# Norm weights as one value per partition behind the transposes, and pooling matrices kept on chip, in a two-block transformer kernel

## The reference, cut to what matters

```python
def first_block(x, c, ...):                      # two layers
    mod = cond @ w_ada[l] + b_ada[l]             # sh1, sc1, g1, sh2, sc2, g2
    h = rms_norm(x, norm1_g[l]) * (1.0 + sc1) + sh1
    proj = h @ w_in[l]                           # pooled part p, and q, k, v
    pooled = windowed_means(p) - p               # windows 2, 4, 8, 16
    pool_out = einsum('bsgc,gcd->bsgd', pooled, pool_w[l]) * pool_scale[l]
    y = rms_norm(concat(pool_out, attn_out), per half of 512) * mix_norm_g[l]
    x = x + g1 * (y @ w_out[l])
    h2 = rms_norm(x, norm2_g[l]) * (1.0 + sc2) + sh2
    x = x + g2 * peer_ffn(h2, ...)               # 128 of 16384 experts a token
def second_block(x, ...):                        # two layers
    proj = rms_norm(x, norm1_g_2[l]) @ w_in_2[l]
    mix = concat(rms_norm(y_a, out_g_mla), y_b, rms_norm(y_c, out_g_swa), rms_norm(y_d, out_g_na))
    x = x + mix @ w_out_2[l]
    x = x + relu(rms_norm(x, norm2_g_2[l]) @ w_up[l])**2 @ w_down[l]
    # at the end rms_norm(x, final_norm_g)
```

## Time and profile before

| | |
|---|---|
| time, median of 3 runs | 2333.84 us (2329.98 to 2336.41) |
| the profiled execution: time, span | 2331.16 us, 2329.4 us |
| PE busy | 2084.4 us (89%) |
| DVE busy | 1346.7 us (58%) |
| ACT busy | 820.0 us (35%) |
| POOL busy | 613.9 us (26%) |
| bytes moved by DMA | 760.73 MB, mean 327 GB/s |

### The profile page before, as it was taken

How to read it: one execution, slowest core, us unless ns; L and a number is a source line. 1 busy time by engine, 2 the same in 40 slices (tenths; PEclk the granted TensorE clock), 3 DMA queues, 4 the chain that set the end, 5 groups by cost and what they waited for, 6 DMA issues and landing times.

```text
span 2329.4 us, 24219 instructions
## 1 busy us (share of the span) xinstructions
PE 2084.4 (89%) x8172; PEld 1235.6 (53%) x8172; DVE 1346.7 (58%) x3055; ACT 820.0 (35%) x2346; POOL 613.9 (26%) x564
## 2 busy tenths in 40 slices
PE   6888998888989888999888888889989999999998
PEld 5554554434545434655433343436756667766665
DVE  2237766985767677776776676754533323444323
ACT  2214643554454344463443344442420001331000
POOL 1124534334334443433444344430000000000000
PEclk9999999999999899999999999999999999989999
DMA  9999999999999999999999999994342442242430
GB/s 374 365 408 426 426 426 427 427 426 427 426 427 411 427 427 417 427 426 427 420 426 403 426 427 427 420 423 169 127 181 109 184 184 77 109 162 93 190 142 18
DMA packets 106848, 760.73 MB, mean 327 GB/s; under 512 B 12114, under 2 KB 12386, under 8 KB 15843
## 3 DMA queue, kind: packets, MB, share of 16 engines
q0 software_dynamic: 80640, 587.24, 60.3%
q1 hardware_dynamic: 26084, 171.94, 18.5%
HBM read 758.08 MB, written 1.05 MB: 326 GB/s over the span
## 4 chain that ended last, share of the span: by engine, by line
PE 52%; DMA 25%; DVE 14%; ACT 6%; issue 2%; POOL 0%; DVEq 0%; ACTq 0%; POOLq 0%
PE PS L541 51%; DMA BIG<-in_uv,EID 22%; DVE BIG L1716 6%; DMA MOD<-in_uv,EID 2%; ACT DG L1018 1%; DMA BIG<-in_wada 1%; ACT L1224 1%; DVE BIG L1378 1%; DVE BIG L1388 1%; PE PS L653 1%; DVE SC L1464 1%; ACT AV L1018 1%; PE PS L620 1%; DVE BIG L1374 1%; DVE X L1378 1%
## 5 line engine op out<-in xcount | busy, mean ns | idle before, releaser
L541 PE MATMUL PS<-BIG,DG 128*128 128x512 f32 x1820 | 891.9, 628 | 157.6 <-ACT DG L1018 138.2
L1716 DVE CUSTOM_DVE_ANT_0 BIG<-BIG,H 128x1024 f32<-128x1024 f32 x455 | 558.1, 1227 | 321.7 <-DMA BIG<-in_uv,EID 292.0
L481 POOL DMA_INDIRECT BIG<-in_uv,EID x455 | 519.4, 1142 | 738.8 <-PE PS L541 708.2
L541 PEld LDWEIGHTS PS<-BIG,DG 128*128 128x128 f32 x1820 | 334.6, 197 | 615.0 <-ACT DG L1018 298.4
L541 PE MATMUL PS<-HT,BIG 128*128 128x128 f32 (+1 forms) x2304 | 382.2, 322 | 7.9 <-DVE HT L1374 3.5
L541 PEld LDWEIGHTS PS<-HT,BIG 128*128 128x128 f32 x2304 | 348.4, 192 | 74.0 <-issue 46.6
L1224 ACT ACTIVATE AV<-AV 128x1 f32<-128x1 f32 x512 | 103.1, 201 | 635.8 <-DVE AV L1716 632.0
L541 PE MATMUL PS<-BIG,HT 128*128 128x256 f32 (+3 forms) x1216 | 295.9, 400 | 7.8 <-DVE HT L1374 3.6
L541 PEld LDWEIGHTS PS<-BIG,HT 128*128 128x128 f32 x1216 | 227.1, 193 | 74.6 <-issue 48.1
L1378 DVE TENSOR_TENSOR BIG<-BIG 128x256 f32<-128x256 f32 (+2 forms) x176 | 96.2, 546 | 221.7 <-ACT BIG L1359 216.5
L1018 ACT ACTIVATE DG<-CST,AV 128x128 f32<-128x128 f32 x512 | 205.5, 401 | 48.0 <-ACT AV L1018 0.7
(11 more groups left out here) (179 smaller groups left out, 1448.2 us busy)
## 6 DMA issues: line engine op xcount, KB each, us to landing
BIG<-in_wada POOLq DMA_DIRECT2D x43, 1024.0 KB
BIG<-in_wup SPq DMA_DIRECT2D x32, 1024.0 KB, 8.9
BIG<-in_wdn SPq DMA_DIRECT2D x32, 1024.0 KB, 4.8
BIG<-in_win SPq DMA_DIRECT2D x31, 1024.0 KB, 4.9
BIG<-in_wq SPq DMA_DIRECT2D x27, 1024.0 KB
BIG<-in_wout SPq DMA_DIRECT2D x24, 1024.0 KB, 5.4
BIG<-in_uv,EID POOLq DMA_INDIRECT x455
MOD<-in_wada POOLq DMA_DIRECT2D x5, 1024.0 KB
```

Of the source, the lines that this page charges most:

```text
L481: pool.e.indirect_dma_start(out=slot(u), out_offset=None, in_=I[f"uv{l}"], in_offset=bass.IndirectOffsetOnAxis(ap=EID[:, t * 128 + j:t * 1 ...
L541: return pe.e.matmul(dst, a, b, start=start, stop=stop)
L1716: v.e.tensor_tensor_reduce(out=JD, in0=slot(u)[:, 0:1024], in1=H[:, t, :], scale=1.0, scalar=0.0, op0=ALU.mult, op1=ALU.add, accum_out=AV[ ...
```

## The change

Most norm weights no longer stand as rows on all partitions. They come in one small transfer (`in_cols`, 128 x 112) as columns, one value per channel with channels on partitions, and the copies behind a transpose multiply by them, since there the channel is the partition. DVE's norm then needs two operands only (`ts` instead of `stt`). ACT's copy of four 128-wide pieces in one instruction becomes four instructions, each with its own column as scale; its copy of a 256-token section pair becomes two. DVE's copy becomes one `tensor_tensor` with the columns spread along the free dimension. `par1` shrinks to 648 values per partition, `par2` to 516. The first block's second norm weight is multiplied into the modulation: in layer 0 as a row loaded to `JS`, in layer 1 on the small tile `ROWS`. The pooling matrices get a place of their own (`MGB`), loaded once for both layers, and `poolw` one (`PWB`), loaded once a layer. The two operands of the modulation matmuls move from `PARB` to `DG` and `TC`.

```diff
-PAR = 3720
+PAR = 792
...
-P1 = dict(n1=(0, 1024), n2=(1024, 1024), ps=(2048, 512), qg=(2560, 64), kg=(2624, 64), sink=(2688, 8), mg=(2696, 1024))
-P2 = dict(n1=(0, 1024), n2=(1024, 1024), q=(2048, 192), kv=(2240, 128), lam=(2368, 128), sub=(2496, 64), sink=(2560, 4),
-          oa=(2564, 256), oc=(2820, 256), od=(3076, 256))
+P1 = dict(ps=(144, 512), qg=(656, 64), kg=(720, 64), sink=(784, 8))
+P2 = dict(q=(144, 192), kv=(336, 128), lam=(464, 128), sub=(592, 64), sink=(656, 4))
+
+GAINS = dict(mg=(80, 8), n1=(96, 8), n2=(112, 8), mix=(128, 8))
...
-        DG = sb("DG", 4 * 128)[:, :].rearrange("p (b n) -> p b n", b=4)
+        DGS = sb("DG", 4 * 128)[:, :]
+        DG = DGS.rearrange("p (b n) -> p b n", b=4)
...
-        ZC = PARB[:, 384:888].rearrange("p (k m) -> p k m", k=8)
-        CREP = PARB[:, 128:384].rearrange("p (k m) -> p k m", k=8)
+        MGB = sb("MGB", 1536)[:, :]
+        PWB = sb("PWB", 512)[:, :]
+        N2R = sb("N2R", 256)[:, :]
+        ZC = DGS[:, 0:504].rearrange("p (k m) -> p k m", k=8)
+        CREP = TC.rearrange("p (k m) -> p k m", k=8)
...
+        def columns(k, l, c, n=4):
+
+            o, w = GAINS[k]
+            return PARB[:, o + l * w + c:o + l * w + c + n]
...
+        GAIN_OF = {(l, 1): ("mg", l) for l in range(L)} | {(2 + l, w): (("n1", None, "n2")[w], l) for l in range(L) for w in (0, 2)}
...
-                    sp.e.dma_start(PARB[:, 1024:PAR], I["par1"][1, 1024:PAR].partition_broadcast(128)).then_inc(*landed("ld_par", 1))
+                    sp.e.dma_start(PARB[:, 144:PAR], I["par1"][1].partition_broadcast(128)).then_inc(*landed("ld_par", 1))
...
-                        sp.e.dma_start(PARB[:, 1024:PAR], I["par1"][0, 1024:PAR].partition_broadcast(128)).then_inc(*landed("ld_par", 0))
+                        sp.e.dma_start(PARB[:, 144:PAR], I["par1"][0].partition_broadcast(128)).then_inc(*landed("ld_par", 0))
+                        sp.e.dma_start(JS, I["n2"][0].partition_broadcast(128)).then_inc(*landed("ld_n2"))
                 yield from k.to(WHEN["pool"])
-                load(in_w, ("mg", l, t), I[f"mg{t}"], 512 * (t + 1), ("pe.pool", l, t))
-                yield from k.to(WHEN["pw"])
-                load(in_w, ("pw", l, t), I["poolw"][l], 512, ("pe.pw", l, t))
+                if l == 0:
+                    sp.e.dma_start(MGB[:, t * 512:t * 1024 + 512], I[f"mg{t}"]).then_inc(*landed("ld_mg", t))
+                if t == 0:
+                    if l > 0:
+                        sp.wait_ge(*at("pe.pw", 0, 1))
+                    sp.e.dma_start(PWB, I["poolw"][l]).then_inc(*landed("ld_pw", l))
...
-            sp.e.dma_start(PARB[:, 32:80], I["cols"]).then_inc(*landed("ld_cols"))
+            sp.e.dma_start(PARB[:, 32:144], I["cols"]).then_inc(*landed("ld_cols"))
...
+            for g in range(4):
+                sp.e.dma_start(N2R[g * 32 + 16:g * 32 + 20, :], I["n2"][1:2].rearrange("a (b n) -> (a b) n", n=256)).then_inc(
+                    *landed("ld_n2r"))
...
-                sp.e.dma_start(PARB[:, 0:3332], I["par2"][0].partition_broadcast(128)).then_inc(*landed("ld_par2", 0))
+                sp.e.dma_start(PARB[:, 144:660], I["par2"][0].partition_broadcast(128)).then_inc(*landed("ld_par2", 0))
...
-                    sp.e.dma_start(PARB[:, 0:3332], I["par2"][l].partition_broadcast(128)).then_inc(*landed("ld_par2", l))
+                    sp.e.dma_start(PARB[:, 144:660], I["par2"][l].partition_broadcast(128)).then_inc(*landed("ld_par2", l))
...
-            sp.e.dma_start(PARB[:, 0:1024], I["fing"].partition_broadcast(128)).then_inc(*landed("ld_fin"))
+            sp.e.dma_start(G2, I["fing"].partition_broadcast(128)).then_inc(*landed("ld_fin"))
...
-                mg = have(in_w, ("mg", l, t))[:, 0:512 * (t + 1)].rearrange("p (a g s) -> p a g s", a=t + 1, g=4)
+                pe.wait_ge(*at("ld_mg", t))
+                mg = MGB[:, t * 512:t * 1024 + 512].rearrange("p (a g s) -> p a g s", a=t + 1, g=4)
...
-                pw = have(in_w, ("pw", l, t))
+                pe.wait_ge(*at("ld_pw", l))
+                pw = PWB
...
                 a.wait_ge(*at("pe.hT", l, t, which, 0))
-                copy(HT[:, 0:4, t * 128:(t + 1) * 128],
-                     PS[:, singles.where[("hT", l, t, which, 0)], :].rearrange("p (c s) -> p c s", c=4)).then_inc(*up("a.hT", l, t, which))
+                src = PS[:, singles.where[("hT", l, t, which, 0)], :].rearrange("p (c s) -> p c s", c=4)
+                if (l, which) in GAIN_OF:
+                    a.wait_ge(*at("ld_cols"))
+                    g = columns(*GAIN_OF[(l, which)], 0)
+                    for c in range(4):
+                        ins = copy(HT[:, c, t * 128:(t + 1) * 128], src[:, c, :], g[:, c:c + 1])
+                else:
+                    ins = copy(HT[:, 0:4, t * 128:(t + 1) * 128], src)
+                ins.then_inc(*up("a.hT", l, t, which))
...
+                if n == 0:
+                    a.wait_ge(*at("pe.ada", 1, 23))
                 copy(DG[:, n % 4, :], ident, AV[:, j:j + 1]).then_inc(*up("a.diag", p, b - 1))
...
-                copy(HT[:, CHUNK[s] * 2:CHUNK[s] * 2 + 2, :],
-                     PS[:, singles.where[("yT", l, s)], :].rearrange("p (c s) -> p c s", c=2)).then_inc(*up("a.yT", l, s))
+                for c in range(2):
+                    ins = copy(HT[:, CHUNK[s] * 2 + c, :], PS[:, singles.where[("yT", l, s)], c * 256:(c + 1) * 256],
+                               columns("mix", l, CHUNK[s] * 2 + c, 1))
+                ins.then_inc(*up("a.yT", l, s))
...
-                tt(ROWS, PS[:, 2, 0:256], ROWS, ALU.add).then_inc(*up("v.rows"))
+                tt(ROWS, PS[:, 2, 0:256], ROWS, ALU.add).then_inc(*up("v.c"))
+                v.wait_ge(*last("ld_n2r"))
+                stt(ROWS, ROWS, CST[:, C_ONE:C_ONE + 1], N2R, ALU.add, ALU.mult).then_inc(*up("v.rows"))
...
-                                PS[:, singles.where[("hT", l, t, which, 1)], :].rearrange("p (c s) -> p c s", c=4)).then_inc(
-                    *up("v.hT", l, t, which))
+                src = PS[:, singles.where[("hT", l, t, which, 1)], :].rearrange("p (c s) -> p c s", c=4)
+                if (l, which) in GAIN_OF:
+                    g = columns(*GAIN_OF[(l, which)], 4)
+                    ins = tt(HT[:, 4:8, t * 128:(t + 1) * 128], src, bc(g.unsqueeze(2), [128, 4, 128]), ALU.mult)
+                else:
+                    ins = cp(HT[:, 4:8, t * 128:(t + 1) * 128], src)
+                ins.then_inc(*up("v.hT", l, t, which))
...
-                    ins = stt(y, y, s[:, j:j + 1], par1("mg")[:, j * 512:(j + 1) * 512], ALU.mult, ALU.mult)
+                    ins = ts(y, y, s[:, j:j + 1], None, ALU.mult, None)
...
-                    stt(sc2, sc2, 1.0, par1("n2"), ALU.add, ALU.mult).then_inc(*up("v.c"))
+                if (l, t) == (0, 0):
+                    v.wait_ge(*at("ld_n2"))
+                    stt(sc2, sc2, 1.0, JS, ALU.add, ALU.mult).then_inc(*up("v.c"))
...
-                stt(H[:, t, :], X[:, t, :], s, par2("n1"), ALU.mult, ALU.mult).then_inc(*up("v.n1", l, t))
+                ts(H[:, t, :], X[:, t, :], s, None, ALU.mult, None).then_inc(*up("v.n1", l, t))
...
+                v.wait_ge(*at("ld_par2", l))
...
-                cp(HT[:, CHUNK[s] * 2:CHUNK[s] * 2 + 2, :],
-                   PS[:, singles.where[("yT", l, s)], :].rearrange("p (c s) -> p c s", c=2)).then_inc(*up("v.yT", l, s))
+                src = PS[:, singles.where[("yT", l, s)], :].rearrange("p (c s) -> p c s", c=2)
+                dst = HT[:, CHUNK[s] * 2:CHUNK[s] * 2 + 2, :]
+                if s == "d":
+                    tt(dst, src, bc(columns("mix", l, 6, 2).unsqueeze(2), [128, 2, 256]), ALU.mult).then_inc(*up("v.yT", l, s))
+                else:
+                    cp(dst, src).then_inc(*up("v.yT", l, s))
...
-                    ins = stt(Y[:, t, o:o + 256], Y[:, t, o:o + 256], y[:, t:t + 1], par2(gain), ALU.mult, ALU.mult)
+                    ins = ts(Y[:, t, o:o + 256], Y[:, t, o:o + 256], y[:, t:t + 1], None, ALU.mult, None)
...
-                    stt(H[:, t, :], X[:, t, :], s, par2("n2"), ALU.mult, ALU.mult).then_inc(*up("v.n2", l, t))
+                    ts(H[:, t, :], X[:, t, :], s, None, ALU.mult, None).then_inc(*up("v.n2", l, t))
...
-                        stt(X[:, t, :], X[:, t, :], s, PARB[:, 0:1024], ALU.mult, ALU.mult).then_inc(*up("v.fin", t))
+                        stt(X[:, t, :], X[:, t, :], s, G2, ALU.mult, ALU.mult).then_inc(*up("v.fin", t))
...
+    cst[16:20, C_ONE] = 1
...
-    o["cols"] = np.ascontiguousarray(np.concatenate([first, a["norm1_g"].reshape(L * 8, 128)], axis=0).T)
-    par = np.concatenate([a["norm1_g"], a["norm2_g"], a["pool_scale"], a["q_norm_g"], a["k_norm_g"], a["attn_sinks"],
-                          a["mix_norm_g"]], axis=1)
+    gains = [a[k].reshape(L * 8, 128) for k in ("norm1_g", "mix_norm_g", "norm1_g_2", "norm2_g_2")]
+    parts = np.concatenate([a["out_g_mla_2"], np.ones((L, 256), f), a["out_g_swa_2"], a["out_g_na_2"]], axis=1)
```

(20 more changed lines are left out.)

3 lines of the change are left out of this document (1 added, 2 removed).

## The result

The changed kernel takes 2317.12 us, the median of 11 executions (2313.11 to 2329.55), against 2335.22 us for the kernel before (11 executions). The medians are 18.1 us apart. The ratio of the two kernels is 0.9928, with a 95% interval of 0.991 to 0.9946, which is 17 us (13 to 21 us). The forecast was 10.2 us less and 2323.6 us, with a range that began at 2320.0: the direction was right, the size was not.

The account below looks back on a forecast made before the run. DMA bytes were taken to bound the gather loop, PE's list the second block. Loop -8.9 and second block -1.3 make -10.2 us, from the median 2333.84 to 2323.6 us; whole range 2320 to 2329.

Parts of the forecast that it names:

- The loop: Gather loop, paced by full DMA engines: 3712 KB fewer bytes at 426 GB/s make it 8.9 us shorter.
- PE waits for no output weight: Rival, loop: layer 1's late first output weight stalls PE in both tiles, 2349.6 us at 55 us landing; 3%.
- the bytes are not lost: Rival, loop: part of the freed transfer time becomes idle engines, only 3.1 us go, 2326.7 us; 14%.
- The copies: ACT's four copies for one before the wide layer: 1.13 us, hidden, 0 us; rival at 1.51 us: 2327.2, 12%.
- section c: Second block: ACT's 512-column copy becomes two of 256 and PE waits for it, +0.24 us per layer, +0.5 us.
- Sum -1.8 us: Second block, tile 0 norms: 0.53 us before the wide layer and 0.36 at layer start, each twice.
- −1.3: Second block in all: norms -1.8 us plus section c's copies +0.5 us.
- I take 0 for it: Start: 512 KB fewer bytes gain 0 because DMA idles at 80 to 120 us; 1.2 us as the bound.
- The rival "More": The start's 512 KB count too and layer starts gain fully: -1.5 us, 2322.1 us; 8%.

Follow-up runs that it names:

- a2: Changed kernel with 14 extra transfers of 256 KB spread over the gather loop, into a tile nobody reads: 2326.5 us (12 executions).
- b2: Kernel before with two-operand norms in both blocks, all transfers as before: 2329.8 us (5 executions), ratio 0.9958.
- b3: Changed kernel with the three-operand form back in all its two-operand norms, transfers and copies as changed: 2327.1 us (6 executions), ratio 0.9953.
- b1: Kernel before, unaltered, timed and profiled a second time: 2335.3 us (12 executions).
- c1: Kernel before with only the two operands of the modulation matmuls moved from PARB to TC and DG: 2336.9 us (12 executions).
- e2: Kernel before with four small loads (1 KB packets) added ahead of the first projection weight: one execution, first gather at 167.7 us.
- e3: Kernel before with the transfer of columns twice as wide (128 x 96): one execution, first gather at 171.7 us.
- c3: Changed kernel with DVE's HT copy ahead of two additions at layer 1's start, and TensorE waiting per HT quarter before the wide layer: 2316.4 us, ratio 0.9922.
- d4: Changed kernel with one more, unread two-operand DVE norm in front of the norm ahead of the wide layer: 2323.1 us (12 executions), ratio 0.9944.
- a3: Changed kernel with the pooling matrices loaded through the ring for every tile, as before: 2324.2 us (12 executions), ratio 0.9942.
- a1: Changed kernel, unaltered, run again as reference: 2317.4 us (6 executions), ratio 0.9924; its profiled execution took 2330.82 us.
- a4: Changed kernel with three extra row transfers of 256 KB each in the start: 2317.5 us (7 executions).
- d1: Changed kernel with the norm rows' input tensors padded to their old length in HBM, transfers reading only the new part: 2316.7 us (6 executions).
- c2: Changed kernel with the three-operand form back in the loop's norm alone: 2316.8 us (7 executions).
- e1: Changed kernel with the four small N2R loads issued behind the first tile's last projection weight, not ahead of the first: one execution, first gather at 167.8 us.

## Why the prediction was wrong

**The loop: right.** Forecast −8.9 us; 1393.6 us in six profiles with the old bytes, 1385.3 in twelve with the new ones: −8.4. a2 confirms the price from the other side. No profile has a DMA share below 1.00 there, PE waits for no output weight in the changed kernel's profile, and the bytes are not lost.

**The copies: right.** 0 in front of the wide layer and +0.24 us for section c came out to 0.02 us. By the formula of the Trainium skill ("VectorE: DVE Perf Modes", section "The TRN2 errata") the estimate for the four was 1.00 us; the trace says 1.14. That the scale operand makes the difference is not shown, since no run has the split without the scale.

**The second block: the step that failed is the norms' term, "Sum -1.8 us".** The waits themselves were right. In the second block and just ahead of it (from 1578 us on), PE waited for the norms 2.7 us before and 0.9 after, 1.8 less (who waited for whom, us, times, longest; first before, then after):

```profile
PE PS L620 <- DVE H L1388: 2.7, 4, 1.0
PE PS L640 <- DVE H L1416: 0.9, 2, 0.4
```

The step took this idle time as the whole price. In the medians the norms are worth 7 to 13 us (b2) and 10 us (b3) instead. Part of it is plain: the second block less half of its half-clock time is 723.1 us in five profiles with the old norms and copies (before, b1, c1, e2, e3; 722.9 to 723.2) and 721.3 in eight with both new (720.6 to 721.7). That is −1.8 us, and 0.6 us more fall between last gather and first transposes (29.1 to 28.5 us): the direct part of the whole change in the second block is −2.4, in place of −1.3.

The rest stays open. Of the 19 us between the means, 8.4 are the loop, 2.4 this direct part and 3.2 the start (below), which leaves some 5. I took these 5 for clock: shorter waits, less half clock in the stage that PE bounds. No run shows that. The profiles have 26 us of half clock in the second block with the old norms and 34 with the new ones, the opposite sign, and c3 took away 2.7 us more of waiting without any multiple. What speaks for it is that b2, b3 and d4 lie above their direct price in the medians, and against reading much into d4 speaks a3, which does so too without a longer wait. The stages are known only for profiled executions, one per kernel, and which stretches fall to half clock differs from one execution to the next, so the question would need many profiles of one kernel.

The half-clock stretch of a1 shown above begins where PE idled 1.47 of 5 us. The Trainium skill ("TensorE: Matmul & The Clock Gate", section "Part 1: The HAM clock gate") tells of a gate that halves the clock when TensorE has been idle. The rows of a1 agree in direction. They add that PE was busy for 3.53 of the 5 us in question, and those of the first profile that the same program can pass the same place at full clock.

**The start: "I take 0 for it" failed too, by 3.2 us.** It was right for the bytes (a4: 768 KB more, and the first gather no later than in others), wrong for the stage. The rival "More" had less time in the start, but by the bytes, which a4 speaks against. The first gather comes at 170.1 us on average in five profiles of the before kind (169.1 to 171.7) and at 166.9 in fourteen with the change (165.5 to 168.3). In all five the 8 KB packets take 342 to 362 ns for most of the time from 18 to 36 us, in all fourteen some 309 ns but for single stretches. 18 us at 367 in place of 422 GB/s are 2.3 us of transfer, so the slow packets are at most 2.3 of the 3.2 us. Operands (c1), layout (d1), bytes (a4) and the wider columns (e3) are not the cause as far as one profile of each can say. What it is stays open.

## What to carry to other kernels

Idle time read from one profile was priced exactly here (1.8 us), and still the medians moved by 7 to 13 us when the norms alone were changed. So test such a price by medians over ten or more executions, of the edit and of an edit that should change nothing of the kind: a3 was one, and came out several us off as well. Before you blame the clock, read it stage by stage in more than one execution. The mean clock over the span rose with the change, but in the profiles it did so in the loop, where it is worth nothing. One program's profiles differed by 17 us. In the stage bound by DMA, half clock (102 or 130 us of it) cost nothing and the shorter norm gave nothing; what counted there were bytes, at the rate of the full engines.

## What the runs showed of the hardware that was not expected

- The same transfers with all DMA engines busy ran at 367 GB/s (before, b1), 390 (c1, e3) and 422 (after, a1) in kernels that differ elsewhere, for 18 us each time. With four small loads ahead of them the kernel before had 420, in one execution.
- The second block's length follows its half-clock time at about one half of it: 730.3 us with 17 (c2), 733.5 with 24 (after), 746.6 with 51 (a1), 747.8 with 53 (a4).
- Whether the clock falls at one certain place, 52 to 54 us into the second block, divides the profiles of the changed kernels: a1, a3, a4 and d1 have it there and take 742 to 748 us, after, a2, c2 and e1 do not and take 730 to 734 us. None of the five with the old norms and copies has it (733 to 740 us).
- Multiplying by columns is free in DVE's copy from PSUM (692 ns with and without). The price of one scale operand on ACT, 94 ns by two one-column instructions of before, fitted for 128 columns too (366 ns measured, 369 estimated).
